# Head selector and row of ones placed ahead of the projection weights in SBUF: the weights start 160 bytes later

## What is computed

```python
h = rmsnorm(x, norm_w[l])
proj = jnp.einsum('bsd,de->bse', h, w_in[l])          # (1024 x 1024) @ (1024 x 6168)
...
y_a = gated_deltanet(gdn_qkv, gdn_z, gdn_b, gdn_a, ...)   # 8 heads of 64, chunks of 64 tokens
y_b = forgetting_attention(fox_q, fox_k, fox_v, fox_z, fox_f, ...)   # 8 heads of 64
...
merged = (g_a * jnp.einsum('bsc,cd->bsd', y_a, w_up_gdn[l])
          + g_b * jnp.einsum('bsc,cd->bsd', y_b, w_up_fox[l]))
x = x + jnp.einsum('bsd,de->bse', merged, w_out[l])
...
return rmsnorm(x, final_norm_w)
```

## Time and profile before

| | |
|---|---|
| time, median of 3 runs (lowest, highest) | 943.96 us (942.51, 944.45) |
| the profiled execution, whole | 942.96 us |
| its span, first to last instruction | 941.2 us |
| PE busy in the span | 924.7 us (98%) |
| granted clock of PE, mean | 1.000 |
| DVE / ACT / POOL busy | 610.6 / 472.6 / 19.8 us |

### The profile page before, as it was taken

One profiled execution on the slowest core, in us unless ns is written; L12 is line 12 of the kernel. 1 busy time (PEld: TensorE's weight loads), 2 busy tenths in 40 slices (PEclk: granted clock), 3 DMA queues, 4 the chain that ended last, 5 costly groups with the idle time before them and its releaser, 6 DMA issues.

```text
span 941.2 us, 15988 instructions
## 1 busy us (share of the span) xinstructions
PE 924.7 (98%) x6413; PEld 703.7 (75%) x6413; DVE 610.6 (65%) x984; ACT 472.6 (50%) x846; POOL 19.8 (2%) x29
## 2 busy tenths in 40 slices
PE   7999999999999999999999999999999999999997
PEld 6778787888788876676766666666667888888886
DVE  7587568799999934454486786867863524247262
ACT  7556654632866625532656547466454543334132
POOL 1000002020000000000000000000000000000000
PEclk9999999999999999999999999999999999999999
DMA  7011451249323393322553325234124332223162
GB/s 251 24 49 45 113 166 45 69 170 209 92 91 112 113 262 87 102 75 90 135 187 92 112 101 169 90 111 126 34 69 167 93 98 66 79 112 112 24 207 83
DMA packets 114576, 104.35 MB, mean 111 GB/s; under 512 B 33144, under 2 KB 94720, under 8 KB 114120
## 3 DMA queue, kind: packets, MB, share of 16 engines
q1 hardware_dynamic: 103112, 80.53, 31.1%
q10 hardware_dynamic: 10240, 18.62, 5.4%
q0 software_dynamic: 1152, 4.19, 1.4%
HBM read 76.32 MB, written 27.00 MB: 110 GB/s over the span
## 4 chain that ended last, share of the span: by engine, by line
PE 45%; DVE 3%; ACT 1%; DMA 1%; issue 1%; SPq 0%; DVEq 0%; ACTq 0%
PE pj L2296 6%; PE pj L2298 5%; PE pj L2297 5%; PE pc L2429 4%; PE pa L2395 3%; PE pa L2364 1%; PE pj L2307 1%; PE pj L2309 1%; PE pj L2308 1%; PE pb L2455 1%; PE pj L2567 1%; PE pj L2566 1%; PE pj L2565 1%; PE pb L2444 1%; DVE pa L2028 1%; PE pa L2399 1%
## 5 line engine op out<-in xcount | busy, mean ns | idle before, releaser
L147 PE MATMUL pj<-h_hi,w_hi 128*128 128x512 f32 x504 | 203.8, 404 | 0.5 <-DVE w_lo L135 0.5
L148 PE MATMUL pj<-h_lo,w_hi 128*128 128x512 f32 x504 | 196.9, 391 | 0.0
L149 PE MATMUL pj<-h_hi,w_lo 128*128 128x512 f32 x504 | 196.6, 390 | 0.0
L147 PEld LDWEIGHTS pj<-h_hi,w_hi 128*128 128x128 f32 x504 | 94.5, 188 | 23.9 <-issue 1.1
L149 PEld LDWEIGHTS pj<-h_hi,w_lo 128*128 128x128 f32 x504 | 94.6, 188 | 20.4
L148 PEld LDWEIGHTS pj<-h_lo,w_hi 128*128 128x128 f32 x504 | 94.7, 188 | 17.9 <-issue 0.2
L2296 PE MATMUL pj<-h_hi,w_hi 128*128 128x512 f32 x248 | 101.4, 409 | 0.3 <-PEq L327 0.3
L2297 PE MATMUL pj<-h_lo,w_hi 128*128 128x512 f32 x248 | 96.9, 391 | 0.0
L2298 PE MATMUL pj<-h_hi,w_lo 128*128 128x512 f32 x248 | 96.8, 390 | 0.0
L2296 PEld LDWEIGHTS pj<-h_hi,w_hi 128*128 128x128 f32 x248 | 46.5, 188 | 19.6 <-issue 10.1
L601 ACT ACTIVATE xc<-pj 128x512 f32<-128x512 f32 x39 | 23.3, 597 | 72.4 <-PE pj L149 71.8
(11 more groups left out here) (377 smaller groups left out, 1869.5 us busy)
## 6 DMA issues: line engine op xcount, KB each, us to landing
w_raw<-in_w_in SPq DMA_DIRECT2D x48, 512.0 KB, 4.4
fox_scratch<-xc ACTq DMA_DIRECT2D x39, 256.0 KB, 2.7
qkv<-in_x SPq DMA_DIRECT2D x8, 512.0 KB, 5.8
fa<-rows_scratch POOLq DMA_DIRECT2D x8, 512.0 KB, 4.8
rv<-fr_scratch SPq DMA_DIRECT2D x16, 256.0 KB, 3.9
ma<-m_scratch SPq DMA_DIRECT2D x8, 512.0 KB, 3.9
rv<-in_w_out SPq DMA_DIRECT2D x8, 512.0 KB, 3.8
w_raw<-in_x SPq DMA_DIRECT2D x8, 512.0 KB, 4.4
```

The source lines that it names most:

```text
L147: nc.tensor.matmul(o, w_hi[:, slot, k], h_hi[:, k, cols], start=(k == 0), stop=False)
L148: nc.tensor.matmul(o, w_hi[:, slot, k], h_lo[:, k, cols], start=False, stop=False)
L149: last = nc.tensor.matmul(o, w_lo[:, slot, k], h_hi[:, k, cols], start=False, stop=(k == KT - 1))
```

## The change

`sel` (128 x 32 values, the selector that sums squares by head, stationary operand of two small groups of products) and `onesr` (one column of ones, broadcast as a stationary operand) are declared ahead of `w_raw` instead of behind `vecs`. They take 128 and 32 bytes. So `w_raw`, `w_hi`, `w_lo`, `ident`, `blk_ones`, `cst` and `vecs` start 160 bytes later (`w_raw` at 82208, `w_hi` at 90400, `w_lo` at 98592), at 288 past a multiple of 512 and 32 past a multiple of 64; `sel` now starts at 82048 and `onesr` at 82176. `spare` and all behind it stay where they were, and so do `h_hi` and `h_lo`. No instruction is added, taken away or moved, and no wait changes.

```diff
         h_hi = sb("h_hi", [P, KT, S], F32R)
         h_lo = sb("h_lo", [P, KT, S], F32R)
+        sel = sb("sel", [P, 32])
+        onesr = sb("onesr", [P, 1], F32R)
         w_raw = sb("w_raw", [P, 2, KT, P])
         w_hi = sb("w_hi", [P, 2, KT, P], F32R)
         w_lo = sb("w_lo", [P, 2, KT, P], F32R)
...
         sgn, bias_raw, bias_s, alog_raw, coef = (vecs[:, 5 + n:6 + n] for n in range(5))
-        sel = sb("sel", [P, 32])
-        onesr = sb("onesr", [P, 1], F32R)
         sb("spare", [P, 8])
         tmp = sb("tmp", [P, S])
```

## The result

| | before | after |
|---|---|---|
| median of the runs (lowest, highest) | 943.57 us (942.51, 944.45) | 952.97 us (952.58, 953.37) |
| span of the profiled execution | 941.2 us | 951.6 us |
| ratio, 95% interval | | 1.0109 (1.0097 to 1.0121) |

The account below looks back on a forecast made before the run. PE's product pace was taken to bound the kernel; terms of 0 on PE, DVE, ACT and transfers left the span at 941.2 us and the profiled execution at 942.96, median 1.0 above, 943.9 us; range 938.0 to 950.0.

Parts of the forecast that it names:

- What bounds the kernel: PE's pace of products sets the time; 2256 projection products at 226.7 ns are 511 us, 54% of the span.
- DVE, ACT, transfers, small products: Work beside the projection: DVE splits 4 to 5 ns more each, hidden; ACT the same; transfers 0 to 1 us; small products 0.
- PE, the projection: 2256 float32r products with moved weights: pace stays at 226.7 ns, cost 0.
- The upper bound for the steady pace: Projection in steady running: an eighth of the 13.4 ns not streaming, 1.7 ns per product, 3.8 us.
- First rival: Weight rows straddling 64-byte pieces slow PE's projection: 945.3 or 949.1 us, harsh form with doubled loads 954.9; chance 0.21.
- Second rival: Projection operands clash on the same low address and the shift parts them: faster, down to 913.7 us; chance 0.15.
- The third rival: Weight transfers write part pieces at other cost or collide more: 0 to 1 us, 944.9 at most; shares the forecast's 0.64.

Follow-up runs that it names:

- the stretches: Whole computation left out, only runs of 96 matmuls with operand offsets varied: float32r products of 512 columns 226.9 ns at 256/0 bytes, 233.2 at 32/0.

## Why the prediction was wrong, point by point

**What bounds the kernel** held: the time is the pace of PE's products, and PE waited nowhere longer. The count, 2256 products, was the right lever; the 72 products of 512 columns in lines 1041 to 1043, whose weights moved too, are missing from it, which is 0.5 us at most.

**DVE, ACT, transfers, small products** held. The neighbour rows gave the right costs: 1220 ns for DVE's split and 1059 for ACT's after the change, and with `w_raw` alone off its place 942.86 us. The small products with `ident` and `blk_ones` were not measured by themselves; the growth of the excess leaves nothing for them. Taking `state` in the earlier trace rows as the witness for the projection did not hold: it is float32, and float32 doesn't pay in the stretches either.

**PE, the projection** is the step that failed. I took 0 because three placements in the earlier trace rows had the same 226.7 ns, and read that as "the pace doesn't care where the operands lie". Their distances were 0, 0 and 256 bytes. All three are the same point of the variable that counts, and the text even noted that stationary and moving operand agree modulo 128 in all of them, without drawing the conclusion that the trace held a single sample. What the runs showed in its place: at a distance of 160 bytes each back-to-back product takes 233.3 ns, 6.7 more, and that is 10.8 us where I had put 0. The upper bound for the steady pace, 1.7 ns per product, was too small by a factor of four. It came from a picture (nine pieces of 64 bytes instead of eight) and from no row, and was used as if it bounded other pictures too.

**First rival.** Its direction was right, and so was what should show it: the pace of lines 2296 to 2298 rose and the output product kept 226.7. Its mechanism was not. A shift of 64 bytes straddles nothing and costs the same, and a shift of 160 bytes of both operands straddles and costs nothing in the projection. Its two prices, 949.1 and 954.9, lie on either side of the 953.0, and the range cut between them at 950.

**Second rival.** It had the right variable, the relation of the two addresses, and the wrong side of it: I supposed equality to be the clash, and it is the placement that runs at 226.7, in every case but the one with both operands 4 bytes off. The argument against it, that the moving operand sweeps through all addresses anyway, fell with it.

**The third rival** is excluded by the kernel with `w_raw` alone.

**The rule weighed.** The Trainium skill ("SBUF — State Buffer", section "Door 1: The DMA port swizzle") has lines of 16 bytes as the grain at which reading costs; by it the shift of ten lines was free. The runs show a cost at 32, 64, 96, 128 and 160 bytes, all whole lines, so for a float32r product the measurement decides against drawing that conclusion from it. The 215.8 ns of the Trainium skill ("TensorE: Matmul & The Clock Gate", section "Back-to-back issue gap") appeared in no stretch; 226.7 was the least for 512 columns. The section gives it for an isolated product, and the second rival took it for the pace of a stream.

The excess of each kernel less that of before accounts for the measured change within 1.4 us (both columns in us):

| kernel | excess less 3.9 us | median less its before |
|---|---|---|
| the change | 10.8 | 9.4 |
| weights 160 on, `w_raw` unmoved | 10.9 | 9.9 |
| `w_raw` 160 on, weights 256 | -0.1 | 0.2 |
| weights 64 on | 10.7 | 9.7 |
| `w_hi` 160 on, `w_lo` 256 | 6.5 | 6.5 |
| weights 128 on | 8.9 | 8.6 |
| weights 192 on | 2.7 | 2.1 |
| weights 256 on | 0.0 | 0.5 |
| all 160 on | 2.6 | 4.0 |
| tokens 160 on, weights 256 | 14.9 | 14.7 |

The pace in these kernels is that of the stretches. The mean over the gate tiles from 720 to 830 us is 233.3 ns with the weights 64 or 160 on, 232.4 with 128, 228.9 with 192, 226.8 with 256, and 234.2 at distance 96.

**What stays open** is what happens inside PE, and why equal offsets of 4 bytes are slow. That two operand streams read at once get into each other's way is suggested, since the effect depends on their distance and comes in locked patterns, but it is argued, not shown. No version beat the kernel before: distance 0 is the floor of all that was tried.

## What to carry to other kernels

Where float32r products of 512 columns set the time, put stationary and moving operand at the same place modulo 256 bytes, for every pair that meets (seen for places at multiples of 32 bytes; 4 bytes on both sides was slow), and pad small tiles so that they don't shift a large one; here a misplaced pair cost 3% of the pace and 1% of the kernel, and 96 bytes more of small tiles ahead of the weights took it back. When several rows agree, ask in which variable they differ before taking them as evidence that it doesn't matter: three placements that are equal modulo 256 are one sample. And a bound that comes from one picture of the mechanism bounds only that picture.

## What the runs showed that I had not expected

- The pace of back-to-back float32r products depends on the distance of the two operands' addresses: 226.7 ns at 0 and 256 bytes (one exception: both 4 bytes off, 233.5), 228.3 to 234.2 ns at nearly all others, at the full granted clock.
- For other distances the pace is one of several locked patterns, chosen also by what ran before: 252 bytes at 226.7 or 233.2 ns, 448 at 228.9 or 233.3.
- It is a matter of type and shape, as far as distance 64 shows: float32 products of 512 columns don't have it, nor float32r ones of 128 columns; at 256 columns distance 64 was 2.2 ns faster than 0.
- The load of the weights of a projection tile is shown at 188 ns before and after the change, so the loss can't be seen in the durations of loads, only in the distance from start to start.
